# Four schedule shifts and a smaller operand in a two-block network: layer norm, planner credit, softmax normalisation, state-space step

## The reference, cut to what matters

```python
# forgetting attention, per head
s = q @ k.T * scale + c[:, None] - c[None, :]      # c: cumulative log forget gate
p = softmax(where(mask, s, -1e30))                 # normalised by its row sum
o = p @ v
```

```python
z, xbc, dt_raw, q, k, v, g_ssd, g_att = split(rmsnorm(h) @ w_in)
xbc = silu(causal_dwconv(xbc)); x, b, c = split(xbc)
dt = softplus(dt_raw + dt_bias) * valid
cs = cumsum(dt * a);  xdt = x * dt[..., None]
y = (c @ b.T * exp(cs_t - cs_s) * causal) @ xdt + carried state + d_skip * x
y = group_rmsnorm(y * silu(z)) ;  att = swa_sink_attention(q, k, v)
h += (sigmoid(g_ssd) * (y @ w_ssd) + sigmoid(g_att) * (att @ w_att)) @ w_out
h += (silu(gate) * up) @ w_down
```

## Time and profile before

| what | before |
|---|---|
| median of 3 runs | 1601.69 us (1601.33 to 1601.81) |
| the profiled execution | 1601.69 us |
| its span on the core | 1599.9 us |
| granted TensorE clock | 1.000 in the whole span |
| TensorE busy | 1580.1 us (99%) |
| VectorE busy | 1130.4 us (71%) |
| ScalarE busy | 921.0 us (58%) |
| POOL busy | 153.2 us (10%) |
| DMA | 266.52 MB, mean 167 GB/s |

### The profile page before, as it was taken

One profiled execution on the slowest core, in us unless ns is written; L12 is line 12 of the kernel. 1 busy time (PEld: TensorE's weight loads), 2 busy tenths in 40 slices (PEclk: granted clock), 3 DMA queues, 4 the chain that ended last, 5 costly groups with the idle time before them and its releaser, 6 DMA issues.

```text
span 1599.9 us, 31022 instructions
## 1 busy us (share of the span) xinstructions
PE 1580.1 (99%) x12570; PEld 1542.5 (96%) x12570; DVE 1130.4 (71%) x2416; ACT 921.0 (58%) x1988; POOL 153.2 (10%) x162
## 2 busy tenths in 40 slices
PE   9999999999999999999999999999999999999998
PEld 9999999999999999999999999989999989999986
DVE  7554578787655888557468875597549997788862
ACT  5444356475443765447557554466766887567653
POOL 4000000000000000000000000102343753100000
PEclk9999999999999999999999999999999999999999
DMA  9554555555455555564265555654354335555551
GB/s 291 176 174 156 187 168 168 176 159 176 161 171 189 173 168 176 172 203 134 88 199 163 182 177 175 193 166 131 120 171 155 110 106 173 182 187 185 185 183 55
DMA packets 251390, 266.52 MB, mean 167 GB/s; under 512 B 4763, under 2 KB 246753, under 8 KB 251248
## 3 DMA queue, kind: packets, MB, share of 16 engines
q1 hardware_dynamic: 249600, 260.72, 50.9%
q0 software_dynamic: 1648, 3.81, 0.9%
HBM read 263.42 MB, written 1.09 MB: 165 GB/s over the span
## 4 chain that ended last, share of the span: by engine, by line
PE 89%; DVE 7%; ACT 3%; issue 1%; DVEq 0%; ACTq 0%
PE ps L1015 53%; PE ps L1017 26%; DVE wl L2179 2%; PE ps L980 1%; PE ps L979 1%; PE ps L978 1%; ACT wh L1473 1%; PE ps L770 1%; DVE CY L2145 1%; PE ps L617 0%; PE ps L755 0%; DVE CY L2267 0%; DVE R L1799 0%; DVE XC L1759 0%; PE ps L788 0%
## 5 line engine op out<-in xcount | busy, mean ns | idle before, releaser
L2179 DVE TENSOR_TENSOR wl<-raw,wh 128x512 fp32r<-128x512 f32 (+1 forms) x968 | 640.2, 711 | 277.6 <-ACT wh L1473 271.7
L1473 ACT ACTIVATE wh<-raw 128x512 fp32r<-128x512 f32 (+1 forms) x1004 | 551.2, 611 | 200.0 <-PE ps L1015 174.0
L1015 PE MATMUL ps<-XH,wh 128*128 128x258 f32 (+3 forms) x2464 | 616.9, 287 | 4.0 <-ACT XH L1109 3.5
L1017 PE MATMUL ps<-XH,wl 128*128 128x258 f32 (+3 forms) x2464 | 613.8, 285 | 0.0
L1015 PEld LDWEIGHTS ps<-XH,wh 128*128 128x128 f32 x2464 | 465.9, 189 | 7.2 <-issue 5.2
L1017 PEld LDWEIGHTS ps<-XH,wl 128*128 128x128 f32 x2464 | 465.1, 189 | 0.1
L1015 PE MATMUL ps<-XL,wh 128*128 128x258 f32 (+3 forms) x2464 | 333.6, 287 | 0.5 <-DVE XL L1882 0.5
L1015 PEld LDWEIGHTS ps<-XL,wh 128*128 128x128 f32 x2464 | 315.0, 189 | 1.8 <-DVE XL L1882 1.3
L1017 PE MATMUL ps<-HH,wl 128*128 128x272 f32 (+1 forms) x704 | 173.4, 284 | 0.0
L1015 PE MATMUL ps<-HH,wh 128*128 128x272 f32 (+1 forms) x704 | 173.4, 285 | 0.0
L1017 PEld LDWEIGHTS ps<-HH,wl 128*128 128x128 f32 x704 | 132.4, 188 | 0.0
(11 more groups left out here) (444 smaller groups left out, 2041.4 us busy)
## 6 DMA issues: line engine op xcount, KB each, us to landing
raw<-in_ffn_wg SPq DMA_DIRECT2D x44, 1024.0 KB, 5.4
raw<-in_ffn_wu SPq DMA_DIRECT2D x44, 1024.0 KB, 5.4
raw<-in_w_in SPq DMA_DIRECT2D x33, 1024.0 KB, 5.3
raw<-in_ffn_wd SPq DMA_DIRECT2D x32, 1024.0 KB, 5.3
raw<-in_w_ffn_in SPq DMA_DIRECT2D x22, 1024.0 KB, 5.2
raw<-in_ffn_wd SPq DMA_DIRECT2D x16, 768.0 KB, 4.6
raw<-in_conv_w_in SPq DMA_DIRECT2D x12, 1024.0 KB, 5.1
raw<-in_w_ffn_out SPq DMA_DIRECT2D x11, 1024.0 KB, 4.9
```

The source lines that it names most:

```text
L1015: mm = e.matmul(o, hi[:, k, c], xk, start=begin, stop=stop)
L1017: e.matmul(o, lo[:, k, c], xk, start=False, stop=False)
L1473: e.activation(wh[u.n % NH][:, c], raw[u.n % NR][:, c], ACT.Copy).then_inc(s_hi, 1)
L2179: e.tensor_tensor(wl[u.n % NR][:, c], raw[u.n % NR][:, c], wh[u.n % NH][:, c].bitcast(F32), ALU.subtract).then_inc(s_lo, 1)
```

## The change

There are five edits. (1) In the fourth layer norm TensorE's matmul of the variance comes five steps earlier, which puts it 8 of the large matmuls earlier in TensorE's list, and five empty steps are put behind it, so that nothing after it moves. (2) The planner's credit ahead of the q2 units begins at 0.0 and not at -0.6, so the steps run from there on come a little earlier in the stream of units. (3) The forgetting attention's normalisation moves from VectorE to POOL (`pool_normalise`). (4) POOL's product EX by CBM is one instruction of 804 elements, and TensorE waits for it once. (5) XDT is made by two instructions, 128 x 256 and 16 x 128; its last third is cleared once for each buffer at c = 0 and 1 on VectorE (`s_xdz`), and the clearing of DTT goes.

```diff
--- before.py
+++ after.py
@@ -400,7 +400,7 @@
     s_dc, s_sp2, s_dt, s_na, s_nega, s_cum2 = (sem(n) for n in ("dc", "sp2", "dt", "na", "nega", "cum2"))
     s_csh, s_csl, s_dT, s_dtt = sem("csh"), sem("csl"), sem("dT"), sem("dtt")
     s_cv, s_ctap, s_th, s_cz = sem("cv"), sem("ctap"), sem("th"), sem("cz")
-    s_cb1, s_cbm, s_xt2, s_xd = (sem(n) for n in ("cb1", "cbm", "xt2", "xd"))
+    s_cb1, s_cbm, s_xt2, s_xd, s_xdz = (sem(n) for n in ("cb1", "cbm", "xt2", "xd", "xdz"))
     s_eb, s_er, s_ee, s_em, s_y, s_yb, s_yz = (sem(n) for n in ("eb", "er", "ee", "em", "y", "yb", "yz"))
     s_bd, s_b2, s_d2, s_r2, s_x2, s_m2x = (sem(n) for n in ("bd", "b2", "d2", "r2", "x2", "m2x"))
     s_gsq, s_gadd, s_gsum, s_gn, s_yh, s_yl = (sem(n) for n in ("gsq", "gadd", "gsum", "gn", "yh", "yl"))
@@ -530,7 +530,7 @@
     P.queue(1)
     P.drain("rs6")
     P.queue(19)
-    P.rate, P.credit = 4.2, -0.6
+    P.rate, P.credit = 4.2, 0.0
     for j in range(4):
         P.group(("q2", j), W_IN, KD, Q0 + 256 * j, 2, two(s_cr, 27 + 2 * j))
     P.ring = (0, 2)
@@ -658,11 +658,11 @@
     def pe_ln(e, i, n0, res):
         pe_mean(e, i, n0)
         yield
-        yield from idle(8 + 20)
+        yield from idle(8 + 15)
         e.wait_ge(s_qa, 4 * i + 4)
         e.matmul(PS[6][:, n0:T], mean1[:], R[:, 0, n0:T], start=True, stop=True).then_inc(s_var, 1)
         yield
-        yield from idle(12 + 8 * res)
+        yield from idle(17 + 8 * res)
 
     def pe_turn(e, o, p):
 
@@ -778,10 +778,8 @@
         else:
             e.wait_ge(s_m2x, 1)
         e.wait_ge(s_xd, c + 1)
-        e.wait_ge(s_em, 2 * c + 1)
+        e.wait_ge(s_em, c + 1)
         for n, (x0, x1) in enumerate(((144, NEX), (0, 144), (0, 16))):
-            if n == 1:
-                e.wait_ge(s_em, 2 * c + 2)
             for par in range(2):
                 h = 2 * c + par
                 M = EX[c % 2][:, par, x0:x1] if n < 2 else E16[:, 16 * h:16 * h + 16]
@@ -1923,10 +1921,6 @@
             if h > 1:
                 e.wait_ge(s_pn, 2 * (h - 2) + 2)
             e.reciprocal(fa.RC[i][:, 1:3], fa.SM[i][:, 1:3]).then_inc(s_rc, 1)
-            e.wait_ge(s_rc, h + 1)
-            for q in (2, 1):
-                p = fa.P[h % 3][:, COLS[q][0]:COLS[q][1]]
-                e.tensor_scalar(p, p, fa.RC[i][:, q:q + 1], None, ALU.mult).then_inc(s_pn, 1)
             yield
 
     def dve_swa_out(e, r):
@@ -2081,14 +2075,21 @@
         for c in range(16):
             if c > 1:
                 dve_ssd_y(e, c - 2)
+            else:
+                e.memset(XDT[c][:, 2, :], 0.0).then_inc(s_xdz, 1)
             e.wait_ge(s_xt2, c + 1)
+            if c < 2:
+                e.wait_ge(s_xdz, c + 1)
             if c == 0:
                 e.wait_ge(s_dtt, 4)
             if c > 1:
                 e.wait_ge(s_y, 2 * (c - 2) + 2)
-            o = XDT[c % 2][:].rearrange("p t (h d) -> p t h d", h=2)
-            e.tensor_tensor(o, PS[6][:, 0:384].rearrange("p (t h d) -> p t h d", t=3, h=2),
-                            DTT[:, :, 2 * c:2 * c + 2].unsqueeze(3).to_broadcast([128, 3, 2, 64]),
+            o = XDT[c % 2][:, 0:2, :].rearrange("p t (h d) -> p t h d", h=2)
+            e.tensor_tensor(o, PS[6][:, 0:256].rearrange("p (t h d) -> p t h d", t=2, h=2),
+                            DTT[:, 0:2, 2 * c:2 * c + 2].unsqueeze(3).to_broadcast([128, 2, 2, 64]), ALU.mult)
+            e.tensor_tensor(XDT[c % 2][0:16, 2, :].rearrange("p (h d) -> p h d", h=2),
+                            PS[6][0:16, 256:384].rearrange("p (h d) -> p h d", h=2),
+                            DTT[0:16, 2, 2 * c:2 * c + 2].unsqueeze(2).to_broadcast([16, 2, 64]),
                             ALU.mult).then_inc(s_xd, 1)
             yield
             yield from idle(c % 2 == 0 and c < 14)
@@ -2529,7 +2530,12 @@
         e.dma_start(scratch, SMK).then_inc(s_b, 16)
         yield
         yield from idle(50)
-        yield from idle(8 * 4 + 2 * 2)
+        for h in range(10):
+            yield from idle(2)
+            if h < 8:
+                yield
+                pool_normalise(e, fa, h)
+                yield
         yield from idle(19 + 1 + 1 + 19)
         for r in range(9):
             yield from idle(4)
@@ -2555,9 +2561,8 @@
                 pool_ssd_y(e, c - 2)
             yield
             e.wait_ge(s_ee, c + 1)
-            for x0, x1 in ((144, NEX), (0, 144)):
-                e.tensor_tensor(EX[c % 2][:, :, x0:x1], EX[c % 2][:, :, x0:x1],
-                                CBM[:, c // 4, x0:x1].unsqueeze(1).to_broadcast([128, 2, x1 - x0]), ALU.mult).then_inc(s_em, 1)
+            e.tensor_tensor(EX[c % 2][:], EX[c % 2][:], CBM[:, c // 4, 0:NEX].unsqueeze(1).to_broadcast([128, 2, NEX]),
+                            ALU.mult).then_inc(s_em, 1)
             yield
             yield from idle(2 * (c % 2 == 0 and c < 14) + (c > 6) + (c > 13))
         pool_ssd_y(e, 14)
@@ -2566,6 +2571,13 @@
         pool_ssd_y(e, 15)
         yield
         yield from idle(12 + 4 + 1)
+
+    def pool_normalise(e, sm, h):
+        i, Pt = h % 2, sm.P[h % 3]
+        e.wait_ge(s_rc, h + 1)
+        for q in (2, 1):
+            c0, c1 = COLS[q]
+            e.tensor_scalar(Pt[:, c0:c1], Pt[:, c0:c1], sm.RC[i][:, q:q + 1], None, ALU.mult).then_inc(s_pn, 1)
 
     def pool_ssd_y(e, c):
         e.wait_ge(s_yb, c + 1)
@@ -2665,7 +2677,6 @@
         e.dma_start(B0[:], shifted(STRIP + 271, 16, 16)).then_inc(s_b, 16)
         e.memset(VN[:, 2, :], 0.0)
         e.memset(E16[:], 0.0)
-        e.memset(DTT[:, 2, :], 0.0)
         e.memset(SPB[:, :, 416:544], 0.0).then_inc(s_spz, 1)
         group("kv2")
         group("dt")
```

## The result

| | before | after |
|---|---|---|
| median | 1601.75 us (1601.33 to 1604.0) | 1611.82 us (1610.96 to 1612.09) |
| the profiled execution, its span | 1601.69, 1599.9 us | 1611.84, 1610.1 us |
| TensorE, VectorE, ScalarE, POOL busy | 1580.1, 1130.4, 921.0, 153.2 us | 1581.2, 1123.0, 920.9, 169.8 us |

The ratio is 1.0058 (95% interval 1.0046 to 1.0069): 10 us slower, where 2.3 were forecast with 1607.0 as the upper end. TensorE does the same work and is busy 1.1 us longer; the other 9 us are waits.

The account below looks back on a forecast made before the run. TensorE, busy 1580.1 of 1599.9 us, was taken as the bound, with VectorE setting the pace in the state-space stage. 0.1 + 0.95 + 0.3 + 0.8 = 2.15 on 1601.69 gave 1603.8, put at 1604.0; range 1601.0 to 1607.0.

Parts of the forecast that it names:

- wait and refund: Fourth layer norm: TensorE waits 1.0 us longer at the variance matmul and gets it all back at XL; +0.1.
- margins: Forgetting attention: time before TensorE must wait for POOL, 0.73 us at head 0, 0.51 at 7, 1.39 at 6, others over 3.
- I take 1.1: Forgetting attention: POOL's time in us for the normalisation pair, near the middle between 0.55 and 1.57; costs +0.95.
- upper end of 1.57: Forgetting attention: POOL's pair in us if priced by the line of its two-tensor products; costs 2.1 us.
- has slack: Forgetting attention: POOL's products may slow VectorE's splits for 8 × 1.1 us, but VectorE has slack there.
- rival A: Forgetting attention: POOL works at line rate, pair about 0.55 us, the move costs nothing; +1.2 in all, 1602.9; chance 0.17.
- +0.3 for ZD and DTA: Credit change: TensorE waits 0.6 us at ZD, 0.4 more at DTA, partly given back; together +0.3 (0 to +0.6).
- scores, exponentials and sums come earlier too: Sliding-window attention: TensorE comes 0.5 us earlier, but its producers do too; put at 0 (up to +0.6).
- margin of 0.33 at the first pair: Sliding-window attention: POOL ends at 1093.30, TensorE turns at 1093.63, the nearest margin there; other pairs 0.3 to 1.3 us.
- +0.065 at each c: State-space stage: XDT by two instructions occupies VectorE 0.54 us in place of 0.48, 16 times, +1.0.
- VectorE has +1.4 more: State-space stage: VectorE's extra time from split XDT and clearings, of which 0.8 (0 to 1.6) reaches TensorE, waiting for YB.
- Rival C: POOL's pair at 1.57 us costs 2.1, VectorE's 1.4 in the state-space stage passes whole; +3.9, 1605.6; chance 0.25.

Follow-up runs that it names:

- m1: Separate kernel, nothing of the reference: POOL products alone, then beside VectorE streams from SBUF, PSUM or both; POOL's pair 1.56 us alone, 2.75 beside SBUF work.
- e9: Kernel before with only the credit at 0.0, plus VectorE's sum and reciprocal one step earlier in the sliding-window attention; 1603.25 against 1602.06 us.
- e1: Kernel before with only the forgetting attention's normalisation moved to POOL; 1606.83 against 1601.89 us, ratio 1.0029.
- e13: Kernel before with only the XDT change, its 16 x 128 instruction left out, clearings and 128 x 256 kept; 1602.22 us, ratio 1.0004.
- e2: Kernel before with only the credit ahead of the q2 units at 0.0 in place of -0.6; 1605.17 us, ratio 1.0019.
- e3: Kernel before with only XDT made by two instructions and its two clearings; 1603.95 us, ratio 1.0012.
- e11: Kernel before with credit -1.2 for the q2 units, given back before the sliding-window attention; median 1603.62 us, lowest 1601.89.
- e12: Kernel before with EX merged into one instruction and e11's credit, nothing else; 1603.67 us, ratio 1.0007, lowest 1601.69.
- e6: Kernel before with only the credit moved the other way, to -1.2 from -0.6; 1602.69 us, ratio 1.0006.

## Why the prediction was wrong

Forecast were +2.3 us, measured +10.1. Three terms of the sum failed, one in each stage.

- **Edit 1** (+0.1): right, wait and refund included.
- **Edit 3** (+0.95, measured +3.8 to +4.1): margins, start and the three heads were right; the step that failed is "I take 1.1". The pair's price at rest is 1.56 us, and the middle had no row behind it. Its premise, that a product by a scalar lies between a MEMSET and a product of two tensors, fell too: at rest, by m1's 1.23 and 0.75, the line of the two-tensor products gives only 1.16 us for 272 and 144. That the prediction's upper end of 1.57 is so near is chance, since the rows that it came from, 1510 and 974 ns, hold POOL's waits beside VectorE. Above that the pair lay beside VectorE's splits at exactly the heads that count, and 2.48 and 1.93 were over the upper end of 1.57. By the prediction's own margins 1.57 gives 2.1 us, so of the loss beyond 0.95 some 1.1 are the price at rest and 1.7 the wait beside the splits. The sentence that VectorE "has slack" there thought of VectorE's loss and not of POOL's. The Trainium skill, "GPSIMD Engine Reference", section 4.1 Engine selection, has one-input work at roughly line rate; rival A stood on it. The measurement differs: one input costs 0.94 us for 272 columns in m1, where two inputs cost 0.75 for 288.
- **Edit 2** (+0.3 for ZD and DTA, measured +0.5; 0 for the sliding-window attention, measured +2.8): the first part was well sized. The failed step is "scores, exponentials and sums come earlier too". They come earlier each on its own engine, against its own splits; ScalarE's exponentials moved past a wh, VectorE's sum didn't move past the split that needs it. The margin of 0.33 at the first pair was read correctly, and the sum being 1.2 us late ate it; TensorE waited 2.1 us at three pairs, where the prediction had no new wait. With the sum moved (e9) these waits go to 0.2 and the loss of edit 2 from 3.3 to 1.2, of which 0.8 in the stage stays without an explanation.
- **Edits 4 and 5** (+0.8 together, measured +2.1 for edit 5 alone and −0.3, no change, for edit 4 alone): that the merged EX costs nothing was right, +0.065 at each c too. The step that failed is "VectorE has +1.4 more", of which 0.8 were let through as a longer wait for YB. That wait stayed at 4.3 us. What came was a wait for POOL's EX, 1.1 us alone and 1.6 in the changed kernel: the 0.065 moved VectorE's split from 0.31 to 0.38 us behind the start of POOL's YB, and now and then POOL lost its turn, for 2.2 us at the most. Besides, TensorE's wait for XDT at c = 1 is 0.6 longer, by the clearings, for which 0.35 were put.
- **Rival C** had the sign, and of the places the forgetting attention and the state-space stage; its 1605.6 was still 6 us short. Its price for the pair was again that of a POOL at rest, and it had nothing for the sliding-window attention. The Trainium skill, "GPSIMD Engine Reference", section 8 Key points, names contention with VectorE's instructions of two SBUF inputs; e1's 2.47 and m1's 2.75 against 1.56 agree. I cited it and put the price on VectorE alone.

## What to carry to other kernels

Price an instruction that goes to POOL beside what VectorE does in that stretch, and in both directions: its own time, plus one wait per instruction for VectorE's work in SBUF (0.45 to 0.69 us each in m1), and a longer one where a turn is lost. When a planner shifts steps, check for each engine pair whether a step passed a piece that the other engine's list still has ahead of it. And what matters is only the margin at the consumer: five of eight heads could move at no cost, three cost it all.

## What the runs showed of the hardware

- The turn between POOL and VectorE is taken per instruction and seems to depend on hundredths of a microsecond. Measured for c = 0 to 13 in every trace, to the nanosecond, is the time from the start of POOL's YB to VectorE's next instruction with both inputs in SBUF. At 0.17 to 0.18 us (10 rows, all of e13) and at 0.30 to 0.32 (113 rows) POOL always kept its 0.74 us or little more. At 0.367 to 0.378 it kept it in all 20 rows. At 0.380 to 0.383 it kept it in 3 of 12, and in the other 9 took 1.66 to 2.97: it ended 0.6 after VectorE's run broke off, which was after one instruction (1.66), three (2.35) or four (2.96). All the rows from 0.367 to 0.383 are of runs with the XDT in two instructions. Why the later comer wins, and whether these few nanoseconds decide it or only go with it, is open.
- The half-clock spell: in e1's profile the granted clock over three microseconds was 0.57,

```profile
1078.00:1081.00 3.00, 3.00 (x15) 2.37 (x12) 2.17 (x5) 0.56 (x3) 0.00 (x0) 0.57 0.00 0
```

  with 0.50, or 1.2 in place of 2.4 GHz, from 1079 to 1081. TensorE had waited 1.2 us for DTA just before, up to 1077.0. The profiles of e2 and e3 have the spell too, and their waits at DTA are 0.6 and 0.9, hardly other than the 0.8 in the profile of before, which has no spell. These three profiles are of executions in the longer group, the others of the shorter; the other executions are told apart by their time alone. So counted, 26 of 117 executions of the kernel before have it, 4 of 8 of e1, and 8 of 11 of e11 and of e12, where TensorE waits 1.1 us for BD near 1079; of e6, with 0.7 there, none of 11. What tips it was not tried.
